# Adaptive-norm modulation of a trunk layer: two vectors moved from VectorE to column-tiled TensorE matmuls, with the start of the kernel reordered

## What is computed

```
cond = silu(c)
mod = cond @ w_ada + b_ada                 # (1024) @ (1024, 6144)
sh1, sc1, gt1, sh2, sc2, gt2 = split(mod, 6)
h = rms_norm(x, g_pre_mix) * (1 + sc1) + sh1
proj = h @ w_in                            # (2048, 1024) @ (1024, 3072)
y = concat(conv_module(...), hgrn2(...)) @ w_out
x = x + gt1 * rms_norm(y, g_post_mix)
h = rms_norm(x, g_pre_ffn) * (1 + sc2) + sh2
x = x + gt2 * rms_norm(hier_moe(h), g_post_ffn)
```

## Time and profile before

| | us |
|---|---|
| median of 3 runs | 1696.66 (1694.56 to 1696.83) |
| span of the profiled execution | 1691.3 |
| PE busy | 1543.5 (91%) |
| DVE busy | 1233.8 (73%) |
| ACT busy | 873.8 (52%) |
| first projection matmul of block 0 starts | 63.88 |
| block 0's projection ends, the mean starts | 216.67 |

### The profile page before, as it was taken

How to read it: one execution, slowest core, us unless ns; L and a number is a source line. 1 busy time by engine, 2 the same in 40 slices (tenths; PEclk the granted TensorE clock), 3 DMA queues, 4 the chain that set the end, 5 groups by cost and what they waited for, 6 DMA issues and landing times. The chain is left out here.

```text
span 1691.3 us, 23716 instructions
## 1 busy us (share of the span) xinstructions
PE 1543.5 (91%) x7340; PEld 1130.4 (67%) x7342; DVE 1233.8 (73%) x1950; ACT 873.8 (52%) x1529; POOL 367.2 (22%) x395
## 2 busy tenths in 40 slices
PE   2699989999999999999999999847999999999974
PEld 2588846688956788855889766525667767677641
DVE  4589776479885498875497973486688778887737
ACT  2322363423384423474324263246688778887746
POOL 1000000100001000001000011014466667665640
PEclk9999998999999999999999999859999999999997
DMA  9342343233322333332332453169999998789959
GB/s 333 120 149 78 123 156 143 75 100 100 89 99 88 100 100 100 113 100 75 88 99 77 182 156 99 74 241 326 357 299 286 325 290 247 201 247 283 276 114 381
DMA packets 200420, 291.25 MB, mean 172 GB/s; under 512 B 10558, under 2 KB 158171, under 8 KB 200346
## 3 DMA queue, kind: packets, MB, share of 16 engines
q1 hardware_dynamic: 170720, 197.15, 34.0%
q0 software_dynamic: 29360, 92.99, 20.0%
q10 hardware_dynamic: 266, 0.14, 0.0%
HBM read 240.42 MB, written 59.26 MB: 177 GB/s over the span
## 5 line engine op out<-in xcount | busy, mean ns | idle before, releaser
L979 DVE SCALAR_TENSOR_TENSOR cv<-late_rows,taps,cv 128x512 f32<-128x512 f32 x480 | 321.7, 744 | 0.1
L1896 DVE TENSOR_TENSOR w_rest<-wgu,w_high 128x1024 fp32r<-128x1024 f32 x192 | 233.8, 1221 | 89.8 <-ACT w_high L1819 86.4
L1819 ACT ACTIVATE w_high<-wgu 128x1024 fp32r x192 | 201.7, 1054 | 97.0 <-PE pgu L1764 73.3
L497 PE MATMUL bank<-wo,yT 128*128 128x512 f32 x512 | 224.2, 594 | 3.6 <-ACT hT L683 2.5
L468 PE MATMUL bank<-hT_high,tiles_operand 128*128 128x512 f32 x512 | 204.3, 399 | 9.6 <-DVE hT_operand L952 8.5
L469 PE MATMUL bank<-hT_operand,tiles_operand 128*128 128x512 f32 x512 | 203.6, 398 | 0.0
L470 PE MATMUL bank<-hT_high,win_operand 128*128 128x512 f32 x512 | 203.6, 398 | 0.0
L497 PEld LDWEIGHTS bank<-wo,yT 128*128 128x128 f32 x512 | 95.7, 190 | 118.3 <-issue 116.3
L1774 PE MATMUL py<-wd,hTe 128*128 x384 | 172.7, 592 | 1.8 <-DVE hTe L1919 0.9
L1762 PE MATMUL pgu<-w_high,x_high 128*128 128x512 f32 x384 | 156.2, 407 | 3.8 <-DVE x_rest L1911 3.8
L1763 PE MATMUL pgu<-w_rest,x_high 128*128 128x512 f32 x384 | 151.4, 394 | 0.0
(11 more groups left out here) (369 smaller groups left out, 2824.9 us busy)
## 6 DMA issues: line engine op xcount, KB each, us to landing
win<-w_in_in SPq DMA_DIRECT2D x64, 512.0 KB, 5.0
wgu<-w_gate_in SPq DMA_DIRECT2D x32, 1024.0 KB
wgu<-w_up_in SPq DMA_DIRECT2D x32, 1024.0 KB
wd<-w_down_in SPq DMA_DIRECT2D x32, 1024.0 KB
win<-w_in_in SPq DMA_DIRECT2D x16, 1024.0 KB, 5.1
wo<-w_ada_in POOLq DMA_DIRECT2D x6, 2048.0 KB, 9.5
y_dram<-zeros POOLq DMA_DIRECT2D x17, 512.0 KB, 5.7
tiles<-x_in POOLq DMA_DIRECT2D x16, 512.0 KB, 6.1
```

What stands on the lines that cost most here:

```text
L497: last = nc.tensor.matmul(out[:], yT[:, w % 2, k, :], wo[:, k, half * 512:(half + 1) * 512], start=(k == 0), stop=(k == KD - 1))
L979: ins = V.scalar_tensor_tensor(out=cv[:, j], in0=u[:, j, w:w + T], scalar=tap, in1=cv[:, j], op0=ALU.mult, op1=ALU.add)
L1819: A(w_high[:, QK * q:QK * q + QK, :], c.wgu[:, bass.ds(slot, 1), QK * q:QK * q + QK, :].rearrange("p a k n -> p (a k) n"), ACT.Copy).then_ ...
L1896: V.tensor_tensor(w_rest[:, part, :], c.wgu[:, bass.ds(slot, 1), part, :].rearrange("p a k n -> p (a k) n"), w_high[:, part, :].bitcast(F3 ...
```

## The change

- **Vectors.** The twelve small loads are parted. Three of them (`c`, `b_ada`, `g_pre_mix`) go first on SP's queue, ahead of x, with a semaphore of their own, and PE transposes them alone. The other eight and the convolution kernel stay on ACT's queue, land elsewhere (`scr`), and are transposed later.
- **Rows on PE.** Vectors 0, 1, 3 and 4 are wholly made by PE. The stationary operand is now `cond_wide[:, k, :]`, 32 columns of which the first is `cond` and the others zero; slice k of a piece writes PSUM partitions 32k to 32k+31. So the four slices of a half row go to four column groups, and the partial sums stand in four partitions. A piece has as many matmuls as before (8, in 16 records). ACT saves all 128 partitions, and `ada_columns` sums over them. `row_to_column` is gone.
- **DVE** has `ada_sums` only for vectors 2 and 5: the sums of pieces 0 to 3 in the head and of piece 6 in block 0's projection are gone.
- **Order.** In the head PE makes rows 0 and 1, columns 0, the late transposes, row 2, tile 2's transpose, row 3, columns 1, tile 3's transpose. In block 0 rows 6 and 7 both come after n = 8. POOL's loads of the later pieces wait for rows on PE.

```diff
-            def ada_row(outs, p, first, final):
+            def ada_row(outs, p):
+                pe.wait_ge(*ada_load(p))
+                half = p % 2
                 for r in range(2):
                     for k in range(4):
-                        last = nc.tensor.matmul(outs[r][0:1, :], cond[:, 4 * (p % 2) + k:4 * (p % 2) + k + 1],
-                                                ada_slot[slot_of(p)][:, k, r * 512:(r + 1) * 512], start=first and k == 0,
-                                                stop=final and k == 3, skip_group_check=True)
-                last.then_inc(ada_used, 1)
+                        last = nc.tensor.matmul(outs[r][k * GROUP:(k + 1) * GROUP, :], cond_wide[:, 4 * half + k, :],
+                                                ada_slot[slot_of(p)][:, k, r * 512:(r + 1) * 512], start=half == 0,
+                                                stop=half == 1, skip_group_check=True)
+                        if r == 1:
+                            last.then_inc(ada_used, 1)
...
-                    if t == 0 and n == 17:
-                        late_row()
+                    if t == 0 and n == 8:
+                        late_rows()
                     if t == 0 and n == 20:
                         ada_columns(3)
...
+            pe.wait_ge(mask_step, 2)
+            pe.wait_ge(vec_in, 16 * len(EARLY_VECS))
+            nc.tensor.transpose(pS[:, 0:SPLIT_VEC], tmp[0:SPLIT_VEC, 0:P], c.ident[0:SPLIT_VEC, 0:SPLIT_VEC]).then_inc(turned, 1)
+            for i in range(2):
+                turn_in(0, i)
+            pe.wait_ge(cond_ready, 1)
             pe.wait_ge(mask_step, MASK_STEPS)
-            pe.wait_ge(vec_in, 16 * (len(VEC) + 1))
-            nc.tensor.transpose(pS[:, 0:NVEC], tmp[0:NVEC, 0:P], c.ident[0:NVEC, 0:NVEC])
+            ada_row((pD, pT), 0)
+            ada_row((pD, pT), 1)
+            ada_columns(0)
+            pe.wait_ge(vec_late_in, 16 * (len(VEC) - len(EARLY_VECS) + 1))
+            pe.wait_ge(cols_ready, 1)
...
             last.then_inc(turned, 1)
-            for i in range(3):
-                turn_in(0, i)
-            ada_columns(0)
+            pe.wait_ge(col_read, 1)
+            ada_row((pD, pT), 2)
+            turn_in(0, 2)
+            ada_row((pD, pT), 3)
             ada_columns(1)
             turn_in(0, 3)
...
-            load_vectors(act)
+            load_late_vectors(act)
+            act.wait_ge(mask_step, MASK_STEPS)
             act.wait_ge(cols_ready, 1)
+            A(cond_wide[:, 0:KD, 0:1], cond.unsqueeze(2), ACT.Silu)
             A(cond, cond, ACT.Silu).then_inc(cond_ready, 1)
             logs()
+            x_sums(0, 0)
+            x_sums(0, 1)
+            save_row((pD, pT), 1, 0)
+            x_sums(0, 2)
+            x_sums(0, 3)
             act.wait_ge(lb_in, 1)
             A(lbt[:, 1:3], lbt[:, 1:3], ACT.Exp).then_inc(cond_ready, 1)
-            for i in range(NT):
-                x_sums(0, i)
+            save_row((pD, pT), 3, 1)
             split_piece(0, 0)
...
-                if t == 0:
-                    ada_sums(3, (0,))
...
-            ada_sums(0)
-            norm_in(0, 2)
-            norm_in(0, 3)
-            ada_sums(1)
```

More of the change, by code:

```diff
@@ L194, in mixer_phase @@
         ada_load = lambda p: (ada_in[p], 16) if p < 4 else (ada_in[6 if p >= 10 else 4 + p % 2], 16 * ADA_TURN[p])
[L195 removed]
+        ada_acc = {m: c.grow for m in (0, 1, 3, 4)} | {2: yt[:, 0], 5: xt[:, 0]}
         diag = [yt[:, 1, 0:512], yt[:, 1, 512:D]]
@@ L345, in _ @@
             ch = Chain(pool, mask_step)
-            ch.step(nc.gpsimd.memset(c.ident[:], 0.0))
+            ch.link(nc.gpsimd.memset(c.ident[:], 0.0))
+            ch.step(nc.gpsimd.affine_select(out=c.ident[:], in_=c.ident[:], compare_op=ALU.not_equal, fill=1.0,
+                                            base=0, pattern=[[-1, P]], channel_multiplier=1))
+            ch.link(nc.gpsimd.memset(cond_wide[:, 0:KD], 0.0))
             ch.step(nc.gpsimd.memset(c.ones[:], 1.0))
@@ L371, in _ @@
             pool.wait_ge(win_in[1], win_bytes(0, 1))
-            pool.wait_ge(ada_summed, 1)
-            load_ada(pool, 6)
+            for before, p in ((0, 6), (1, 7), (6, 8), (7, 9), (8, 4), (9, 5)):
+                pool.wait_ge(*rows_done(before))
+                load_ada(pool, p)
             pool.wait_ge(ada_summed, 2)
[L375 to L381, removed]
             pool.dma_start(wo[:], ap["w_out"][0].rearrange("(k p) n -> p k n", p=P)).then_inc(wo_in, 16)
@@ L390, in _ @@
         def _(pe):
-            taken = {4: (cols_ready, 1), 5: (cols_ready, 1)}
+            taken = {4: (cols_ready, 2), 5: (cols_ready, 2)}
             def take(kind, i, half, t):
@@ L419, in row_to_column @@
[L419 to L425, removed]
-            def ada_columns(m):
[L429 to L436, removed]
+                        last = nc.tensor.matmul(outs[r][k * GROUP:(k + 1) * GROUP, :], cond_wide[:, 4 * half + k, :],
+                                                ada_slot[slot_of(p)][:, k, r * 512:(r + 1) * 512], start=half == 0,
+                                                stop=half == 1, skip_group_check=True)
@@ L437, in ada_columns, with late_rows @@
+                        if r == 1:
+                            last.then_inc(ada_used, 1)
+            def late_rows():
+                ada_row((pS, pO), 6)
+                ada_row((pS, pO), 7)
+            def ada_columns(m):
+                if m in (2, 5):
+                    pe.wait_ge(ada_summed, {2: 2, 5: 4}[m])
+                else:
+                    pe.wait_ge(row_saved, {0: 2, 1: 4, 3: 6, 4: 8}[m])
                 if m == 5:
                     pe.wait_ge(masked, NB * NT)
-                out = {2: bank[0][:, 0:KD], 5: pS[:, 0:KD]}.get(m, pT[:, m * KD:(m + 1) * KD])
+                out = {4: bank[1][:, 0:KD], 2: bank[0][:, 0:KD], 5: pS[:, 0:KD]}.get(m, pT[:, m * KD:(m + 1) * KD])
@@ L440, in ada_columns @@
                 for j in range(KD):
[L441 to L444, removed]
+                    last = nc.tensor.matmul(out[:, j:j + 1], ada_acc[m][:, j * P:(j + 1) * P], c.ones[:, 0:1],
+                                            start=True, stop=True, skip_group_check=True)
@@ L452, in ada_half, with middle_columns @@
                         pe.wait_ge(*taken[n])
-                pe.wait_ge(*ada_load(p))
-                ada_row(bank[0:2], p, half == 0, half == 1)
+                ada_row(bank[0:2], 8 + half)
+            def middle_columns():
+                ada_columns(4)
+                ada_columns(2)
             def piece_half(t, n):
@@ L639, in steps @@
                     elif kind in FIRST_WORK:
-                        {"ada": ada_half, "columns": lambda: ada_columns(2), "rows": gain_rows, "bias": bias_rows}[kind](*at)
+                        {"ada": ada_half, "columns": middle_columns, "rows": gain_rows, "bias": bias_rows}[kind](*at)
                     elif kind in LAST_WORK:
@@ L749, in gates, with save_row @@
                 logs()
[L751 to L754, removed]
+            def save_row(rows, p, columns):
+                act.wait_ge(*rows_done(p))
+                wait(act, ada_cols_done, columns)
                 for r in range(2):
-                    A(c.grow[0:1, r * 512:(r + 1) * 512], rows[r][0:1, :], ACT.Copy).then_inc(cond_ready, 1)
+                    A(c.grow[:, r * 512:(r + 1) * 512], rows[r][:], ACT.Copy).then_inc(row_saved, 1)
             def log_forget(t, h):
@@ L1243, in _, with save_columns @@
             dve.wait_ge(turned, 1)
+            ch.link(V.tensor_copy(c.cols[:, 0:SPLIT_VEC], pS[:, 0:SPLIT_VEC]))
+            dve.sem_inc(cols_ready, 1)
+            norm_in(0, 0)
+            norm_in(0, 1)
+            def save_columns(m):
+                dve.wait_ge(ada_cols_done, m + 1)
+                ch.link(V.tensor_tensor(m_of(m), pT[:, m * KD:(m + 1) * KD], b_ada_of(m), ALU.add))
+            save_columns(0)
+            dve.sem_inc(col_read, 1)
+            dve.wait_ge(turned, 2)
             ch.step(V.tensor_copy(c.taps[:], pO[:, 0:NCH * CW]))
-            ch.step(V.tensor_copy(c.cols[:], pS[:, 0:NVEC]))
-            ch.sync()
+            ch.link(V.tensor_copy(c.cols[:, SPLIT_VEC:NVEC], pS[:, SPLIT_VEC:NVEC]))
             dve.sem_inc(cols_ready, 1)
```

40 lines of the change are left out of this document (25 added, 15 removed).

## The result

| | before | after |
|---|---|---|
| median of the runs, us | 1695.61 | 1677.16 (1675.42 to 1678.63) |
| span of the profiled execution | 1691.3 | 1673.6 |

What follows compares the result with a forecast made beforehand. PE, busy 91% of the span, was taken as the bound, DVE counting only where PE waits for it. Head 10.5 plus block 0's projection 9.0 gave 19.5 us: 1696.7 - 19.5 = 1677.2 us, range 1671 to 1690.

Steps and rivals of the forecast that it cites:

- The price of a piece: Row pieces on PE: four column groups fully overlapped cost a quarter, 1.7 us at 2.4 GHz, 3.5 at 1.2.
- Rival B: Row pieces: overlap only in program order or of some groups, 9 units, 3.9 us a piece; 1684.7 us; chance 0.13.
- Rival D: Row pieces: no overlap of four groups, 6.9 us a piece, slower at 1700.1 us; chance 0.08.
- The head: Up to the first projection matmul: scale at 41.2 against 51.7, gain 10.5 us, bounds 7.3 to 12.
- Block 0's projection: On PE: rows 6 and 7 gain 3.4, columns 3 4.5, clock 1.1; gain 9.0 us, bounds 5 to 10.
- DVE's last 28 taps begin at 187.3: Block 0's projection: piece 11's split comes 3.4 us earlier, so the taps end at 205.9.
- margin of 1.3 us: Block 0's projection: DVE finishes at 206.4, PE at 207.7, so DVE clears by 1.3 us.
- Block 0's steps: Rows 8 and 9 shrink by 10.4 us on PE, priced at nothing.
- cover by DVE's chain: Block 0's steps: DVE's chain bounds the stretch; PE already waits 3.87 us at its end and will wait longer.
- bounds of +3 and -3: Block 0's steps: gain of 3 us if ACT's next tile starts sooner, loss of 3 if PE's clock stays low.
- After block 0: After the mixer everything starts earlier by the same amount, with no fixed time to meet; priced at zero.
- rival C: Block 0 gives gain back: DVE's taps or step hand-overs bound, or the clock stays low; 1685 us; chance 0.11.

Runs made afterwards that it cites:

- the first and second experiments: Changed kernel with all four slices of a piece in one column group: 1707.0 us; changed kernel with slices as the outer loop: 1679.9 us.
- columns twice: Changed kernel with each of the eight matmuls of columns 3 issued twice: 1674.4 us in one run.

## Why the prediction was right

**The price of a piece, right.** 1.7 us against 1.73 measured. It was read from the overlap of two groups in `outputs` and from the order of starts in `state_sums`; the first and second experiments show both readings. Rival B (9 units) is ruled out. Rival D had the right price for a piece without overlap: it gave 1700.1, and the kernel built so took 1707.0. It had the head 2.0 us longer and the projection 1.4, and they were 6.1 and 5.7 longer. In the head the clock is what it left out, which was low through part of rows 0 and 2; in the projection a part is PE's wait of 1.9 us for DVE.

**The head, 10.5 forecast, 11.9 measured.** The chain of steps was right one by one, down to piece 3's landing. The term mis-sized is the clock: row 1 and columns 0 were taken at 1.2 GHz and ran at 2.4. In the two other profiles they ran at 1.2 GHz as forecast, and the gain was 11.0 and 10.9, so 0.9 us of the 11.9 belong to one execution. The forecast gave the early vectors no price of their own. Left out, they cost 5.4 to 6.3 us.

**Block 0's projection, 9.0 forecast, 5.1 measured: the step that failed.** PE's part came out as sized: its last projection matmuls end 8.8 us earlier in the stage. The step "DVE's last 28 taps begin at 187.3" failed, and with it the margin of 1.3 us. DVE's end came 147.6 us into the stage where 142.5 was forecast, 5.1 us late, and PE waited 3.67 us, then ran the mean partly at the lower clock. There are two causes.
- The step let the split of piece 11 come 3.4 us earlier and forgot what stands on DVE between piece 10's split and piece 11's, a split and twelve taps, 10.2 us without a wait (168.18 to 178.34). With piece 10's split where it was before, 113.0 us into the stage, piece 11's can come at 123.2 at the earliest; 121.2 was forecast.
- Rows 6 and 7, put after n = 8, make the later halves late, piece 10's split among them: 116.2 us into the stage, 3.2 later than before.

The run with the rows after n = 17 undoes the second cause alone. Piece 10's split comes at 112.4 and DVE still works through to the end, at 143.9. That is 1.4 us behind the forecast, so the margin of 1.3 was not there in that kernel either. But PE's last matmul ends there too, and the stage takes 143.9 us, 8.9 less than before: what PE was forecast to save, 9.0, is there once DVE doesn't take it back.

**Block 0's steps, 0 forecast, 2.0 measured.** The cover by DVE's chain is real and incomplete (1.3 us of 10.3); the clock decides the rest. The bounds of +3 and -3 held it.

**After block 0, 0 forecast, -1.3 measured**, all of it in the steps of blocks 1 to 3, whose work the change does not touch; projections, routing and experts moved rigidly. **The total.** These errors, +1.4, -3.9, +2.0 and -1.3, leave the span 1.8 us short of the forecast gain (17.7 for 19.5). One more term brings them back: the median was taken to stay 5.4 us over the profiled span and stood 3.6 over it (1677.16 and 1673.6). That distance is no fixed cost. Each execution of the changed kernel took about 1.8 us more than its own span, and the rest is how fast the profiled execution was beside the median. The range was right for its reasons (rival C, DVE's taps becoming the bound, holds a part of the truth); that the point was met to 0.1 us is luck. Later comparisons gave 0.9916 (0.9884 to 0.9948) and 0.9930 (0.9917 to 0.9943), 14 and 12 us: the sign is beyond doubt, the size is 12 to 19 us.

## What to carry to other kernels

Short-sided f32 matmuls that share a moving size can be set in four column groups by padding the stationary operand to 32 columns and writing to partitions 32k. Here they then cost a quarter, in both loop orders that were run; without that, the same work on PE cost more than it saved. When a saving on the busiest engine is as large as the slack of the next one, follow the next engine's list from its last wait to its end, item by item, and look where inserted work pushes what it waits for. And price a gap or a run of tiny matmuls on PE with what the clock does behind it.

## What was unexpected of the hardware

- Records of other column groups start even where four records of one group stand ahead of them in the program: 1.8 us a piece in both loop orders.
- With identical work, the steps of blocks 1 and 2 took 110.3 us at a mean clock of 1.00 and up to 114.6 at 0.96, those of block 3 148.3 to 156.6 at 0.94 to 0.88, and one kernel (rows after n = 17) showed 148.3 and 156.6 in two profiles. So differences between kernels below some 8 us can't be read from the whole span of one execution of this program. Block 0's projection and steps can: in three profiles of the changed kernel each agreed to 0.1 us, and the projection was 0.5 us longer in a kernel whose edit doesn't touch it (148.15 with rows 8 and 9 in one group). The head differed by 0.9.
- The mean's clock doesn't follow from PE's wait alone. It took 5.40 us behind waits of 3.7 us, 3.70 us behind one of 1.88 (columns twice), and 5.40 us behind one of 1.91 (all pieces in one group).
